# Attention results of three or four jobs side by side in one PSUM bank, copied out together

## The reference

```python
s = (jnp.einsum('bqhc,bkc->bhqk', q_lat, ckv) + jnp.einsum('bqhr,bkr->bhqk', q_rope, krope)) * SM_SCALE
s = jnp.where(mask, s, -jnp.inf)          # prompt: a chunk of 64 queries sees its own and all earlier chunks
p = jax.nn.softmax(s, axis=-1)
o_lat = jnp.einsum('bhqk,bkc->bqhc', p, ckv)
o_attn = jnp.einsum('bqhc,chd->bqhd', o_lat, lw['w_uv']).reshape(B, T, A_HEADS * V_DIM)
```

## Time and profile before

| | |
|---|---|
| median of 3 runs | 2254.7 us (2254.15 to 2259.59) |
| the profiled execution | 2253.61 us |
| its span, first to last instruction | 2251.7 us |
| mean granted clock of TensorE | 0.939 of full |
| busy over the span | PE 1923.4 us (85%), PE weight load 1690.4 (75%), DVE 928.0 (41%), ACT 637.8 (28%), POOL 207.2 (9%) |
| the product with the values, L1867 | 1424 matmuls, 71.1 us busy, 28.1 us of idle time ahead of them |
| the copies, L1424 | 68, of 128 partitions x 64 columns |

### The profile page before, as it was taken

One profiled execution on the slowest core, in us unless ns is written; L12 is line 12 of the kernel. 1 busy time (PEld: TensorE's weight loads), 2 busy tenths in 40 slices (PEclk: granted clock), 3 DMA queues, 4 the chain that ended last, 5 costly groups with the idle time before them and its releaser, 6 DMA issues. The chain is left out here.

```text
span 2251.7 us, 41181 instructions
## 1 busy us (share of the span) xinstructions
PE 1923.4 (85%) x17018; PEld 1690.4 (75%) x17018; DVE 928.0 (41%) x1438; ACT 637.8 (28%) x1269; POOL 207.2 (9%) x287
## 2 busy tenths in 40 slices
PE   4999974288899998898842995999999999999996
PEld 3999952156666766666621983999999999999995
DVE  4222254544454445445419119242334233423347
ACT  5322342033334424434324124212111211111114
POOL 0000000022332322423200000100000000000000
PEclk8999997589999999999976998999999999999998
DMA  7111025610100101000092303111011101110122
GB/s 277 47 37 47 28 61 153 201 52 30 35 18 30 35 19 46 19 18 21 16 351 85 132 22 108 38 57 48 25 42 57 47 20 48 56 48 19 47 108 80
DMA packets 112180, 147.85 MB, mean 66 GB/s; under 512 B 65968, under 2 KB 80944, under 8 KB 111568
## 3 DMA queue, kind: packets, MB, share of 16 engines
q1 hardware_dynamic: 112016, 145.41, 19.8%
HBM read 114.90 MB, written 30.50 MB: 65 GB/s over the span
## 5 line engine op out<-in xcount | busy, mean ns | idle before, releaser
L391 PE MATMUL ps<-hhi,whi 128*128 128x364 f32 (+1 forms) x1728 | 573.9, 332 | 74.0 <-DVE wlo L384 38.1
L391 PE MATMUL ps<-hlo,whi 128*128 128x364 f32 (+1 forms) x1728 | 573.4, 332 | 4.7 <-issue 4.7
L391 PE MATMUL ps<-hhi,wlo 128*128 128x364 f32 (+1 forms) x1728 | 572.9, 332 | 0.0
L391 PEld LDWEIGHTS ps<-hhi,whi 128*128 128x128 f32 x1728 | 329.3, 191 | 75.6 <-issue 58.5
L391 PEld LDWEIGHTS ps<-hhi,wlo 128*128 128x128 f32 x1728 | 329.3, 191 | 5.2 <-issue 5.2
L391 PEld LDWEIGHTS ps<-hlo,whi 128*128 128x128 f32 x1728 | 329.3, 191 | 0.0
L384 DVE TENSOR_TENSOR wlo<-wraw,whi 128x1024 fp32r<-128x1024 f32 x74 | 90.5, 1224 | 505.3 <-ACT whi L380 503.4
L727 POOL TENSOR_TENSOR nlev<-gm,con 64x256 f32<-64x256 f32 x204 | 156.3, 766 | 246.0 <-DVE gm L1323 232.0
L1565 DVE TENSOR_TENSOR acc<-acc,ps 128x364 f32<-128x364 f32 (+1 forms) x240 | 126.5, 531 | 101.9 <-PE ps L1982 101.9
L1982 PE MATMUL ps<-ahi,dhi 128*128 128x364 f32 (+1 forms) x480 | 158.5, 330 | 2.4 <-DVE acc L1565 2.4
L1982 PE MATMUL ps<-alo,dhi 128*128 128x364 f32 (+1 forms) x480 | 157.5, 328 | 0.0
(11 more groups left out here) (214 smaller groups left out, 2514.8 us busy)
## 6 DMA issues: line engine op xcount, KB each, us to landing
wraw<-in_w_tiles SPq DMA_DIRECT2D x72, 512.0 KB, 3.5
late<-in_ada_w SPq DMA_DIRECT2D x8, 2048.0 KB, 9.3
ci<-scan SPq DMA_DIRECT2D x17, 768.0 KB, 4.5
draw<-in_w_down SPq DMA_DIRECT2D x20, 512.0 KB, 3.4
slab<-in_ada_w SPq DMA_DIRECT2D x4, 2048.0 KB, 19.0
scan<-mix SPq DMA_DIRECT2D x12, 512.0 KB, 4.4
x<-in_x_t SPq DMA_DIRECT2D x4, 1456.0 KB, 9.5
x<-x_mid SPq DMA_DIRECT2D x1, 4352.0 KB, 13.3
```

The lines of the kernel that those rows point to most:

```text
L391: mm = nc.tensor.matmul(ps[:, 3 * u + c, 0:n], w[u][:, k, :], x[:, k, a:a + n], start=(k == 0 and w is whi and x is hhi), stop=(k == KD - ...
```

## The change

`OUT_BLOCKS` cuts the job order of a pair into six blocks: chunks 15, 14, 13; chunks 12, 11, 10; the sample; chunks 9, 8, 7, 6; chunks 5, 4, 3, 2; chunks 1, 0. Jobs of a block write their results into bank 5 side by side, 64 columns each, in ascending order of chunks, so that they lie as they do in `oatt`. There is one copy for a block, of 64, 128, 192 or 256 columns, and "out" is emitted only for a block's last job. Only the first product of a block waits for the copy of the block before it. The counts of `o_ev` go from 17 to 6 a pair everywhere.

```diff
+OUT_BLOCKS = [JOB_ORDER[0:3], JOB_ORDER[3:6], [SAMPLE_JOB], JOB_ORDER[7:11], JOB_ORDER[11:15], JOB_ORDER[15:17]]
+OUT_AT = {job: (i, min(block)) for i, block in enumerate(OUT_BLOCKS) for job in block}
...
                 units.append(("values", before, 0))
-                if TURNS[before][0] != job:
+                if TURNS[before][0] != job and any(TURNS[before][0] == x[-1] for x in blocks):
                     out = TURNS[before][0]
             before = x
-    return units + [("out", out, 0), ("values", before, 0), ("out", JOB_ORDER[-1], 0)] + next_keys
+    return units + [("values", before, 0), ("out", JOB_ORDER[-1], 0)] + next_keys
...
             def put_out(job, hp):
-                a = C * job
+                block, low = OUT_AT[job]
+                a, n = C * low, C * len(OUT_BLOCKS[block])
                 dve.wait_ge(o_mm, N_TURNS * hp + T_END[job] + 1)
-                nc.vector.tensor_copy(oatt[:, bass.ds(hp, 1), a:a + C].rearrange("p a b -> p (a b)"), ps[:, 5, 0:C]).then_inc(o_ev, 1)
+                nc.vector.tensor_copy(oatt[:, bass.ds(hp, 1), a:a + n].rearrange("p a b -> p (a b)"), ps[:, 5, 0:n]).then_inc(o_ev, 1)
...
                 pe.wait_ge(t_ev, N_TURNS * hp + x + 1)
-                if t0 == 0:
-                    pe.wait_ge(o_ev, JOBS * hp + JOB_ORDER.index(job) + 1)
+                block, low = OUT_AT[job]
+                if t0 == 0 and job == OUT_BLOCKS[block][0]:
+                    pe.wait_ge(o_ev, len(OUT_BLOCKS) * hp + block + 1)
...
-                        mm = nc.tensor.matmul(ps[r, 5, 0:C], vt[0:rows, at, r], pt[0:rows, x % RING, P * (t - t0) + 64 * e:P * (t - t0) + 64 * e + 64],
+                        mm = nc.tensor.matmul(ps[r, 5, C * (job - low):C * (job - low) + C], vt[0:rows, at, r], pt[0:rows, x % RING, P * (t - t0) + 64 * e:P * (t - t0) + 64 * e + 64],
                                               start=(t == 0), stop=(t == n - 1))
...
-            pe.wait_ge(o_ev, JOBS * PAIRS + 1)
+            pe.wait_ge(o_ev, len(OUT_BLOCKS) * PAIRS + 1)
```

More of the change, by code:

```diff
@@ L90 @@
 assert N_SCORES % 2 == 0 and N_TURNS % RING == 0
+OUT_BLOCKS = [JOB_ORDER[0:3], JOB_ORDER[3:6], [SAMPLE_JOB], JOB_ORDER[7:11], JOB_ORDER[11:15], JOB_ORDER[15:17]]
+OUT_AT = {job: (i, min(block)) for i, block in enumerate(OUT_BLOCKS) for job in block}
+assert all(sorted(x) == list(range(min(x), max(x) + 1)) for x in OUT_BLOCKS)
 def pair_units(first, last):
@@ L98, in pair_units @@
     scored, out, before = 0, None, None
+    blocks = OUT_BLOCKS
     def scores(count):
@@ L619, in _ @@
             sp.dma_start(d["wkv"][1, :, :], state[1][:, :, :].rearrange("p a b -> p (a b)")).then_inc(state_out, 16)
-            sp.wait_ge(o_ev, JOBS * PAIRS + 1)
+            sp.wait_ge(o_ev, len(OUT_BLOCKS) * PAIRS + 1)
             load_slab = lambda n: sp.dma_start(late[n % 2][:, :, :], ada[:, :, 512 * n:512 * n + 512]).then_inc(late_in[n % 2], 16)
@@ L744, in _ @@
                 slot_pool(x, x % 2)
-            pool.wait_ge(o_ev, JOBS * PAIRS + 1)
+            pool.wait_ge(o_ev, len(OUT_BLOCKS) * PAIRS + 1)
             for u in range(2):
@@ L1085, in _ @@
             split_hi(act, OUT_M, 1)
-            act.wait_ge(o_ev, JOBS * PAIRS + 1)
+            act.wait_ge(o_ev, len(OUT_BLOCKS) * PAIRS + 1)
             act.wait_ge(rw_done, KR)
@@ L1491, in _ @@
             gain(3, 40, 0.0)
-            dve.wait_ge(o_ev, JOBS * PAIRS + 1)
+            dve.wait_ge(o_ev, len(OUT_BLOCKS) * PAIRS + 1)
             dve.wait_ge(rw_done, KR)
@@ L1888, in query @@
                 elif l == 1:
-                    pe.wait_ge(o_ev, JOBS * hp + 1)
+                    pe.wait_ge(o_ev, len(OUT_BLOCKS) * hp + 1)
                 else:
```

## The result

| | before | after |
|---|---|---|
| median of the runs, us | 2254.4 (2251.66 to 2259.59, 4 runs) | **2231.7** (2227.45 to 2233.67, 4 runs) |
| profiled execution, us (span) | 2253.6 (2251.7) | 2227.45 (2225.7) |

The ratio of the runs is 0.9894, 95% interval 0.9881 to 0.9908: faster by about 1.1%, the way that was forecast.

A forecast was written before the change was run, and what follows sets the result against it. PE was taken to set the stage's pace, waiting on DVE's queue. 15.9 of removed waits - 1.2 coming back - 1.1 for longer copies + 3.4 of clock = 17.0 us; 2254.7 - 17.0 = 2237.7 us, range 2233 to 2248.

The forecast's parts named there:

- Waits kept and longer copies: Blocks' first products keep 11.8 us of PE waits; wider 192- and 256-column copies on DVE cost 1.1 us.
- Waits removed: Ahead of the products with the values, PE waits for dropped copies go: 15.9 us together.
- the last product's wait: Pair 3's very last product: its 0.36 us wait lies beside the scan's end and brings nothing.
- What is late next: After removed waits at chunk 11 (loop) and chunk 10 (pair 3), PE waits for other work: 1.2 us come back.
- The clock: Half-clock stretches after chunk 0's wait in pairs 1 and 2 go: 3.4 us gained, bounds 0 and 3.4.
- The stage's sum, 17.0: Attention and scan stage: 15.9 - 1.2 - 1.1 + 3.4 = 17.0 us gained.
- by half: Rival: half of the removed waits come back as DVE and ACT lose slack; around 2246 us, chance 0.17.
- gather at the boundaries: Rival: removed waits reappear at block boundaries, so no time is gained; 2255.8 us, chance 0.06.
- The rival "more": A lighter DVE queue also shortens kept waits, 4 to 5 us more; 2233 us and below, chance 0.05.
- The step that failed: PE's register instructions for the dropped waits lie under running matmuls, so removing them gives nothing.
- the luck as which I had written off a gain in the feed-forward part: Sign: the same gain from less feed-forward time would be luck and not this mechanism.

The follow-up runs named there:

- the fourth experiment: Changed kernel plus 44 dummy 64-column copies at the dropped places, each waiting for its job's products and waited for by PE: 2256.89 us, ratio 1.0005.
- the repeated profile: The changed kernel run and profiled once more with nothing altered: median 2232.66 us (5 runs).
- the seventh experiment: Kernel before, attention untouched, with 26 more do-nothing PE instructions where PE waits for `yt`: 2245.36 us, ratio 0.9957.
- the first experiment: Kernel before, except that chunks 1 and 0 share a copy, so only the wait ahead of chunk 0's product goes: 2248.06 us, ratio 0.9969.
- the sixth: Changed kernel with 17 more do-nothing PE instructions where PE waits for `yt`, restoring the earlier program length: 2241.0 us, ratio 0.9935.

## Why the prediction was right and wrong

*Waits kept and longer copies: right.* 11.8 us of kept waits and 1.1 for the longer copies make 12.9; 13.0 were measured. The 192-column copies take 0.348 us and the 256-column ones 0.418 at most (forecast 0.35 and 0.42).

*Waits removed: right.* 28.1 - 13.0 = 15.1 us, against 15.9 - 1.1 + 0.4 (the last product's wait, which counted for nothing) = 15.2. That it is the wait and not the copy is shown by the fourth experiment.

*What is late next: too small.* The wait at L1752 rose by 2.4 us and that of L1760 for ACT from 2.7 to 3.4, some 3 us; other rows fell. At L1752 behind chunk 11 it is 1.20 us in pair 1 and 1.22 in pair 2, where I had 0.9: less of DVE's work moved forward there than I took. From the first to the last product PE's idle time fell by 13.3 us, so 1.8 of the 15.1 came back in all; in the repeated profile 14.2 went and idle time fell by 11.7, so 2.5 came back. I had 1.2.

*The clock: between its bounds, its cause shown in part.* Both stretches of the forecast stand in the two profiles of the unchanged attention (here and, at 798.4 and 958.9, in the seventh experiment) and went in all that drop that wait, the first experiment's included; in the changed kernel other stretches came, so that of the forecast 3.4 us a net 1.7 remain in the first profile (13.6 instead of 17.1 us at half clock) and 3.4 in the repeat (10.2). The fourth experiment has a wait at the same place and the stretch in pair 1 only, so the wait was needed for these stretches but is not always enough. PE's busy time fell by 3.9 us; with 1.7 from the clock, 2.2 of them are not assigned (in the repeat 1.8 of 5.2). The Trainium skill, which the prediction set against this term ("TensorE: Matmul & The Clock Gate", "Loop structure matters more than you think"), says that a copy out of PSUM leaves the clock alone in a loop whose next matmuls follow immediately. Here they did not follow immediately: PE stood still for 1.56 us until the copy was done, and without that wait both stretches were gone. I had read the page for more than it says.

*The stage's sum, 17.0: right, in part by luck,* at 16.4 to 17.2 us in the profiles. 15.1 - 1.8 + 1.7 make 15.0; the other 2.2 are busy time that no term held. Of the rivals, the waits came back by 1.8 to 2.5 us and not by half, and they did not gather at the boundaries (the kept ones grew by 0.2 us at most). The rival "more", 2233 and below, has the number but not its reason: it wanted shorter kept waits.

*The step that failed* is the one that cost the program itself at nothing: "the register instructions for the dropped waits lie under running matmuls: nothing". No run measured their own time, and the stage's sum needs none. But PE's program was 17 instructions shorter behind them, and three loop turns 550 us later lost their second stand: 8.5 us in the profile, 8.3 by the seventh experiment, 8.3 and 9.3 by the sixth (2241.0 against the two medians of the changed kernel, 2232.7 and 2231.7). Nor was it the luck as which I had written off a gain in the feed-forward part. 2254.4 - 17 - 8.5 = 2228.9 is what the terms of the profiles give; the median is 2231.7. The profiled execution of the changed kernel is the fastest of its four runs, and medians of one set give less for the stage: 12.7 us (2241.0 against 2253.7) and 8.3 for the place. The range ended at 2233 since nothing in it stood for a cost outside the stage. The profile of before had the term on show, "issue 4.7" at the one product that never waits; I had read only the stage's rows.

## What to carry to other kernels

Price a shared buffer by whose queue stands between its user and its release: 44 cheap copies that nobody waits for cost some 4 us at most, while 44 turns in DVE's queue cost 15 us of waiting and some clock; three blocks a pair were 8 us better than six. Read the "issue" rows of loops the change doesn't touch, since an edit ahead of a loop moves its head within its 16-KB piece of program: before believing a small gain or loss, pad the program back to its old length and compare. On the engine that bounds, try a loop with few turns written out if its turns show an idle time put down to "issue"; here writing out three turns gave 12.8 us.

## What the runs showed of the hardware

A backward jump of TensorE cost 2.5 to 2.9 us of standing still in every turn of the feed-forward loop; at all three turns of before a 16-KB instruction transfer begins with it. If, by the reading above, the head lies four products ahead of its piece's end, a second stand of 1.1 to 2.3 us follows (nine turns at 4 products; at 5 products 1.5, 0.7 and 1.6), at 11 to 13 products 0 to 0.7. The Trainium skill, page "Runtime: NRT & Kernel Launch", section "Instruction fetch mechanics", says that instructions come in 16-KB blocks and that a taken branch to a page not held stalls on its fetch; these traces agree, with the price above, though none shows whose instructions a transfer carries. It also says that crossing a block's boundary is mostly hidden: that holds here for the written-out loop (idle 0.0), but not right behind a jump.

The granted clock fell at these stands. In every turn of the kernel before, with two stands of 2.8 and 1.3 to 1.7 us and 0.9 to 1.6 us of work between them, it was 1.2 GHz for 6.8 us, from 2.0 to 4.4 us after the first stand began (at the middle turn this was before PE resumed). In both profiles of the changed kernel it was 1.2 GHz for 3.4 us at the first and the last turn and stayed at 2.4 GHz at the middle one. With the loop written out it stayed at 2.4 GHz from 1500 to 2201 us.
